# Five edits of a static job list in a two-layer transformer step: loads and transposes at the start, one late turn of layer 0, the boundary of the layers, who splits twelve weight quarters, and where the last gate's sigmoid stands

## The chip, the cores and the metric

The kernel runs on one core of a Trainium2 chip. The metric is the device time in microseconds (us), as the median of several runs. TensorE (PE in the rows) multiplies and transposes, with its weight loads as PEld; VectorE is DVE, ScalarE is ACT, GpSimd is POOL, and SyncE (SP) issues nearly all transfers.

## What is computed

One inference step of two layers over 512 tokens of a new stream and 8 x 16 tokens of running streams, in float32, with D_MODEL 1024. The first layer has latent attention and differential attention side by side; the second has stick-breaking attention.

```
def _even_layer(x, pos, caches, prm, lam_init):
    h = x @ w_in
    q_lat, ckv, krope, g_mla, dq, dk, dv, g_diff = _split_cols(h, EVEN_SECTIONS)
    ...
    o = jnp.concatenate([o_mla * jax.nn.silu(g_mla), o_diff * jax.nn.silu(g_diff)], axis=-1) @ w_out
    y = _layernorm(ALPHA * x + o, ln_g, ln_b)

def _odd_layer(x, pos, caches, prm):
    q, k, v, g = _split_cols(x @ w_in, (SB_W, SB_W, SB_W, SB_W))
    ...
    o = (o.reshape(b, s, SB_W) * jax.nn.silu(g)) @ w_out
    y = _layernorm(ALPHA * x + o, ln_g, ln_b)

def _sb_core(q, k, v, qpos, kpos):
    z = jnp.einsum('bqhd,bkhd->bhqk', q, k).astype(jnp.float32) * (SB_HD ** -0.5)
    valid = kpos[None, :] < qpos[:, None]
    log_beta = jax.nn.log_sigmoid(z)
    log_rem = jnp.where(valid, jax.nn.log_sigmoid(-z), 0.0)
    later = lax.cumsum(log_rem, axis=3, reverse=True) - log_rem
    a = jnp.where(valid, jnp.exp(log_beta + later), 0.0).astype(v.dtype)
```

## The kernel before

`make_schedule()` writes one list of jobs, a tuple for each. Every engine walks the same list from start to end and does its share of each job, in the order of the list, so a job that waits on an engine holds back all that stands behind it on that engine. Semaphores join the engines. Tokens stand in five tiles of 128: 0 to 3 the prompt, 4 (`S_TILE`) the running streams.

**Products.** A float32 factor is split into a high part (a cast on ACT) and the rest (a subtraction on DVE); a product is three matmuls (high by high, low by high, high by low, line L932). `("xT", layer, t, h)` transposes half h of tile t: four transposes on TensorE (L970), the cast of all four on ACT (L1335), the subtraction on DVE (L1569), which sets the PSUM bank free.

**Weights.** They come in 144 quarters of 128 x 2 x 256 or 128 x 512 words, through three stage buffers. `("cvt", n)`: SP loads quarter n, ACT casts it into `w_hi` (L1345), DVE subtracts into `w_lo` (L1575), and only then does SP load quarter n + 3 in its place. Quarters 128 to 143 are the second layer's output weights, `out100`, `out110`, `out101`, `out111`: the last two digits are the half of the 1024 input rows (k) and the half of the output columns. `w_hi` and `w_lo` hold two sections, so a section may be overwritten only when its last reader is done (`upper_read` is such a flag).

**Banks.** `assign_banks` deals out PSUM banks along the list: `turn0`, `turn1`, `value0`, `proj0` in a ring for most jobs; `pair0` and `pair1` (two banks each) for the attention scores; and `begin` jobs take theirs from a ring of four, which are the two banks of `pair0` (`score0`, `score1`) and the two of `pair1` (`turn2`, `proj1`). A bank is taken when its last user is `drained`.

**Output projections.** `("out", layer, first, t, h)` multiplies tile t with half h of the output weights, in eight k blocks of three matmuls; `("begin", layer, t)` does the first four blocks of the right half ahead. DVE adds the bank to `x_sb` (L1812, L1817); `ln` is then four DVE instructions (L1821 statistics, L1832, L1833, L1835), a power on GpSimd (L905) and the scaling with it on DVE (`shift`, L1846).

**Attention of layer 1.** A step of `stick_pipeline` is the scores of a few heads on a pair of banks, ACT's log-sigmoids (L1435 to L1437), a masked product, scan and product on DVE (L1683, L1687, L1689; the last one drains the pair), ACT's exponential (L1442), transposes on TensorE (`turn`, L1147), and the product with the values. `fills` are the other jobs laid between the steps. `("sig", g, 1)` is ACT's sigmoid of a gate's second half, in three activations of 128 x 640 (L1534 to L1536), and `sigm` the product on DVE and one more activation (L1869, L1540).

## Time and profile before

| | |
|---|---|
| median of 3 runs | 869.32 us (866.99 to 869.53) |
| the profiled execution | 869.3 us, its span 867.5 us |
| TensorE busy | 829.4 us, 96% |
| VectorE, ScalarE, GpSimd busy | 527.5, 413.0, 63.5 us |
| mean granted clock of TensorE | 0.991 |

Each row of a timeline gives the start in us from the span's start, the time taken in us, the engine, the line and operation, what is written and read, the count of alike instructions in a row, and in brackets the idle time ahead and what ended it. Instructions of one engine overlap a little, so the distance of their starts is less than their durations.

### The profile page before, as it was taken

The page shows a single profiled execution, that of the slowest core. Times are in us where ns is not written, and L with a number is a line of the kernel's source. Part 1 is how long each engine was busy: PE and PEld are TensorE (multiplying, and loading weights), DVE is VectorE, ACT ScalarE, POOL GpSimd, SP SyncE. Part 2 cuts the span into 40 slices and gives each one's busy share as a digit, 9 for nine tenths or more (in the row PEclk, how much of TensorE's full clock was granted, in tenths as well). Part 3 has the DMA queues.
Part 4 walks back from the last instruction along what each step waited for, and adds up shares of the span by engine and source line. Part 5 has one row for each costly group of instructions (what it writes and reads, how often), then busy time and mean ns, then how long its engine had stood idle before and what let it go on. Part 6 is the DMA issues. An engine that isn't in the chain of part 4 may idle for free.

```text
span 867.5 us, 17101 instructions
## 1 busy us (share of the span) xinstructions
PE 829.4 (96%) x6676; PEld 707.8 (82%) x6676; DVE 527.5 (61%) x1056; ACT 413.0 (48%) x945; POOL 63.5 (7%) x94
## 2 busy tenths in 40 slices
PE   6999999999999999999999999999999999999994
PEld 6996687878888888677899998888888888877673
DVE  3265346655565657667833466666566776777867
ACT  4233443343444456432224555754675555785710
POOL 2120000000000000001210010001000100000002
PEclk9999999999999999999999999999999999998998
DMA  6631212211323333413133334233333333343203
GB/s 225 152 105 50 61 44 65 64 39 31 129 65 106 105 100 134 139 59 138 49 117 104 117 104 136 88 105 117 114 99 100 118 130 111 100 136 106 73 22 121
DMA packets 67389, 86.25 MB, mean 99 GB/s; under 512 B 6000, under 2 KB 53904, under 8 KB 67312
## 3 DMA queue, kind: packets, MB, share of 16 engines
q1 hardware_dynamic: 63568, 74.47, 27.1%
q0 software_dynamic: 3744, 10.70, 3.9%
q8 instruction: 55, 0.90, 0.4%
q14 instruction: 22, 0.18, 0.1%
HBM read 74.25 MB, written 10.90 MB: 98 GB/s over the span
## 4 chain that ended last, share of the span: by engine, by line
PE 71%; issue 18%; DVE 4%; ACT 3%; POOL 2%; DMA 1%; DVEq 0%; SPq 0%; POOLq 0%; ACTq 0%
PE turn L932 25%; PE pair L932 14%; PE value L932 13%; PE proj L932 11%; PE turn L970 2%; POOL rstd L905 2%; PE turn L1147 1%; PE proj L970 1%; PE value L970 1%; DVE w_lo L1575 1%; PE value L1147 1%; PE proj L1147 1%; PE pair L970 1%; DMA x_sb<-in_x_prompt_dram 0%; ACT w_hi L1345 0%
## 5 line engine op out<-in xcount | busy, mean ns | idle before, releaser
L1575 DVE TENSOR_TENSOR w_lo<-stage,w_hi 128x512 fp32r<-128x512 f32 (+1 forms) x144 | 97.0, 682 | 109.1 <-ACT w_hi L1345 108.9
L932 PE MATMUL turn<-w_hi,xT_hi 128*128 128x256 f32 (+2 forms) x406 | 127.3, 314 | 0.3 <-DVE x_sb L1817 0.3
L932 PE MATMUL turn<-w_hi,xT_lo 128*128 128x256 f32 (+2 forms) x406 | 123.2, 303 | 0.0
L932 PE MATMUL turn<-w_lo,xT_hi 128*128 128x256 f32 (+2 forms) x406 | 123.1, 303 | 0.0
L1345 ACT CAST w_hi<-stage 128x512 fp32r<-128x512 f32 (+1 forms) x144 | 87.2, 615 | 30.0 <-PE turn L932 8.5
L932 PEld LDWEIGHTS turn<-w_hi,xT_hi 128*128 128x128 f32 x406 | 78.1, 192 | 3.6 <-DVE x_sb L1817 0.5
L932 PEld LDWEIGHTS turn<-w_hi,xT_lo 128*128 128x128 f32 x406 | 77.9, 192 | 3.1
L932 PEld LDWEIGHTS turn<-w_lo,xT_hi 128*128 128x128 f32 x406 | 78.2, 193 | 2.7
L932 PE MATMUL value<-w_hi,xT_hi 128*128 128x256 f32 (+2 forms) x196 | 62.8, 320 | 3.0 <-DVE w_lo L1575 3.0
L1425 ACT ACTIVATE work<-pair,peak 128x512 f32<-128x512 f32 (+4 forms) x80 | 41.0, 517 | 45.5 <-DVE peak L1676 45.4
L1687 DVE TENSOR_TENSOR_SCAN probs<-probs 128x512 f32<-128x512 f32 (+4 forms) x80 | 60.9, 794 | 1.6
L932 PE MATMUL value<-w_lo,xT_hi 128*128 128x256 f32 (+2 forms) x196 | 59.9, 306 | 0.0
L932 PE MATMUL value<-w_hi,xT_lo 128*128 128x256 f32 (+2 forms) x196 | 59.9, 305 | 0.0
L932 PE MATMUL turn<-xT_hi,w_hi 128*128 128x320 f32 x176 | 56.0, 318 | 0.0
L932 PE MATMUL turn<-xT_hi,w_lo 128*128 128x320 f32 x176 | 54.4, 309 | 0.0
L932 PE MATMUL turn<-xT_lo,w_hi 128*128 128x320 f32 x176 | 54.4, 309 | 0.0
L932 PE MATMUL proj<-w_hi,xT_hi 128*128 128x256 f32 (+2 forms) x150 | 46.4, 309 | 2.1 <-DVE w_lo L1575 1.3
L932 PE MATMUL proj<-w_lo,xT_hi 128*128 128x256 f32 (+2 forms) x150 | 44.7, 298 | 0.0
L932 PE MATMUL proj<-w_hi,xT_lo 128*128 128x256 f32 (+2 forms) x150 | 44.7, 298 | 0.0
L932 PEld LDWEIGHTS value<-w_hi,xT_hi 128*128 128x128 f32 x196 | 38.1, 195 | 6.2 <-issue 3.1
L1435 ACT ACTIVATE probs<-pair 128x272 f32<-128x272 f32 (+4 forms) x48 | 28.8, 600 | 26.5 <-PE pair L932 26.2
L932 PE MATMUL pair<-w_hi,xT_hi 128*128 128x256 f32 (+2 forms) x128 | 40.4, 316 | 0.8 <-DVE xT_lo L1569 0.8
(527 smaller groups left out, 2024.5 us busy)
## 6 DMA issues: line engine op xcount, KB each, us to landing
stage<-in_w_in_odd_dram SPq DMA_DIRECT2D x64, 256.0 KB, 2.6
stage<-in_w_in_even_dram SPq DMA_DIRECT2D x44, 256.0 KB, 2.8
k_c<-in_cache_sb_k_dram SPq DMA_DIRECT2D x32, 256.0 KB, 3.4
v_c<-in_cache_sb_v_dram SPq DMA_DIRECT2D x32, 256.0 KB, 2.9
x_sb<-in_x_prompt_dram SPq DMA_DIRECT2D x8, 512.0 KB, 4.3
mlaK<-in_cache_diff_k_dram SPq DMA_DIRECT2D x8, 512.0 KB, 3.9
mlaK<-in_cache_diff_v_dram SPq DMA_DIRECT2D x8, 512.0 KB, 4.4
stage<-in_w_out_even_dram SPq DMA_DIRECT2D x16, 256.0 KB, 2.7
```

Of the source, the lines that this page charges most:

```text
L905: nc.gpsimd.tensor_tensor(rstd[:, i, :], mv[:, i, 1:2], minus_half[:, 0:1], ALU.pow).then_inc(pow_out, 1)
L932: return nc.tensor.matmul(o, l, r, start=first, stop=last)
L970: i = nc.tensor.transpose(ps(job)[0:c, c0:c0 + r], src, ident[0:r, 0:r])
L1147: m = nc.tensor.transpose(ps(job)[0:kn, j * P:(j + 1) * P], p[:, k0:k0 + kn], ident[:, :])
L1345: nc.scalar.copy(piece(w_hi[:, sec % 2, k * 512:(k + 1) * 512]), piece(stage[:, n % STAGES, :])).then_inc(hi_done, 1)
L1425: e = nc.scalar.activation(prob(s, i), ps(score)[:, i, 0:width(s)], ACT.Exp, bias=peak[:, r, i:i + 1], accum_out=total[:, r, i:i + 1])
L1435: link(nc.scalar.activation(e, z, ACT.Abs))
L1575: v.tensor_tensor(piece(w_lo[:, sec % 2, words]), piece(stage[:, n % STAGES, :]), piece(w_hi[:, sec % 2, words].bitcast(F32)), ALU.subtrac ...
L1687: i = v.tensor_tensor_scan(c, c, c, 0.0, ALU.add, ALU.max)
```

## The change

1. Start. Tile 0 of the input is loaded as left half, weight quarter 0, right half (with a semaphore of its own, `x_right_in`), quarters 1 and 2, in place of whole tile, quarters 0, 1, 2. The list goes `xT 0 0 0`, `cvt 0`, `xT 0 0 1` in place of both `xT` first. The projection `A` of every tile waits for the transposed right half only at its fifth k block.
2. Turn 42 of layer 0. `cvt 51` and `mcvt 4` (the cast and the subtraction of the fourth output operand, L1349 and L1580) stand behind turn 43's work.
3. Boundary of the layers. `begin` for tiles 0, 1 and 4 now comes first; `ln` and `shift` of the tiles are interleaved with the projections; four `xT` stand in a row ahead of `out 0 2 3 1`, and those of tiles 2 and 3 come behind `k 0 0` and `k 0 1`. `upper_read` is given by `last_lower`, which is `out 0 2 3 1`.
4. Splits. For quarters 128 to 139 the subtraction is GpSimd's, into the same `w_lo`.
5. `sig 3 1` stands one turn later.

```
+POOL_SPLITS = range(QUARTERS * (len(SECTIONS) - 4), QUARTERS * (len(SECTIONS) - 1))
...
-    jobs = layer0(0) + first + [("A", 0, 0)] + layer0(1)
+    jobs = [("xT", 0, 0, 0)] + first[:1] + [("xT", 0, 0, 1)] + first[1:] + [("A", 0, 0)] + layer0(1)
...
-        fills[i].append(bundle)
+        fills[i].append(bundle if i < 42 else bundle[:1])
...
-            fills[i].append([("mcvt", bundle[0][1])])
+            fills[i if i < 42 else i + 1].append([("mcvt", bundle[0][1])] + (bundle[1:] if i == 42 else []))
...
-    jobs += finish(0) + finish(1) + layer1(0) + finish(2) + layer1(1) + finish(3) + coming[:1] + layer1(2) + coming[1:] + finish(S_TILE)
+    jobs += [("begin", 0, 0), ("begin", 0, 1), ("begin", 0, S_TILE), ("out", 0, 2, 0, 1), ("ln", 0, 0), ("out", 0, 2, 1, 1)]
+    jobs += [("shift", 0, 0), ("ln", 0, 1), ("shift", 0, 1), ("out", 0, 2, 2, 1), ("ln", 0, 2)] + layer1(0) + layer1(1)
+    jobs += coming[:1] + [("shift", 0, 2)] + coming[1:3] + [("out", 0, 2, 3, 1)] + coming[3:] + [("ln", 0, 3)]
+    jobs += [("out", 0, 2, S_TILE, 1), ("shift", 0, 3), ("ln", 0, S_TILE), ("shift", 0, S_TILE)]
...
-            keys = [[("k", g, 0)] + layer1(3), [("k", g, 1), ("kT", g, 0)],
+            keys = [[("k", g, 0)] + layer1(2), [("k", g, 1), ("kT", g, 0)] + layer1(3),
...
-              [six[0], [("ocvt", 3), ("sig", g, 1)]], [[("sigm", g, 1)], six[1] + [("ocvt", 2), ("silu", g, 1)] + second[2:]],
+              [six[0], [("ocvt", 3)]], [[("sig", g, 1)], [("sigm", g, 1)] + six[1] + [("ocvt", 2), ("silu", g, 1)] + second[2:]],
...
+        def wait_split(eng, n):
+            if n in POOL_SPLITS:
+                eng.wait_ge(pool_cvt_done, n - POOL_SPLITS.start + 1)
+            else:
+                eng.wait_ge(cvt_done, n + 1 - (len(POOL_SPLITS) if n >= POOL_SPLITS.stop else 0))
...
+            sp.dma_start(x_sb[:, 0, 0:D // 2], x_p[:, 0, 0:D // 2]).then_inc(x_in[0], 16)
+            load_quarter(0)
+            sp.dma_start(x_sb[:, 0, D // 2:], x_p[:, 0, D // 2:]).then_inc(x_right_in, 16)
...
+                elif kind == "cvt" and job[1] in POOL_SPLITS:
+                    n = job[1]
+                    sec, words = n // QUARTERS, slice(n % QUARTERS * 512, (n % QUARTERS + 1) * 512)
+                    pool.wait_ge(hi_done, n + 1)
+                    nc.gpsimd.tensor_tensor(w_lo[:, sec % 2, words], stage[:, n % STAGES, :],
+                                            w_hi[:, sec % 2, words].bitcast(F32), ALU.subtract).then_inc(pool_cvt_done, 1)
...
+                        if job[0] == "A" and k == KD // 2:
+                            wait_drained(pe, ("xT", 0, t, 1))
```

Line numbers of the changed kernel are higher by 19 to 21 for the lines named here (L932 becomes L951, L970 L991, L1147 L1167, L1569 L1589, L1846 L1866).

TensorE at the boundary, before: behind `out 0 2 1 1` on `turn0` stand the transposes of tile 0, then `out 0 2 2 1` on `proj0`, the transposes of tile 1, and `out 0 2 3 1` on `value0`.

```order
L970 MATMUL turn1<-ident,x_sb 128x128 [waits drained_turn1,ln_done]
L970 MATMUL value0<-ident,x_sb 128x128 [waits drained_value0,ln_done]
L932 MATMUL proj0<-w_hi,xT_hi 128x512 [waits ocvt_done,drained_proj0,drained_turn1]
L970 MATMUL turn0<-ident,x_sb 128x128 [waits drained_turn0,ln_done]
L970 MATMUL turn1<-ident,x_sb 128x128 [waits drained_turn1,ln_done]
L932 MATMUL value0<-w_hi,xT_hi 128x512 [waits ocvt_done,drained_value0,drained_proj0]
```

The same place after the change, from `out 0 2 2 1` on `proj0` on.

```order
L951 MATMUL proj0<-w_hi,xT_hi 128x512 [waits ocvt_done,drained_proj0,drained_turn1]
L991 MATMUL turn0<-ident,x_sb 128x128 [waits drained_turn0,ln_done]
L991 MATMUL turn1<-ident,x_sb 128x128 [waits drained_turn1,ln_done]
L991 MATMUL value0<-ident,x_sb 128x128 [waits drained_value0,ln_done]
L991 MATMUL proj0<-ident,x_sb 128x128 [waits drained_proj0,ln_done]
L951 MATMUL turn0<-w_hi,xT_hi 128x512 [waits ocvt_done,drained_turn0,drained_proj0]
```

Four transposed halves now use all four banks of the ring in a row, and `out 0 2 3 1` takes `turn0` again, the first of them.

VectorE at that place after the change, from the addition of `out 0 2 2 1` to that of `out 0 2 3 1`.

```order
L1832 SCALAR_TENSOR_TENSOR x_sb<-x_sb,proj0 128x512 [waits filled_proj0,xres_in2]
L1841 BN_STATS bn<-x_sb 128x6 [waits drained_proj0]
L1852 BN_AGGR mv<-bn 128x2 [waits stats_done,drained_proj0,drained_turn1]
L1853 TENSOR_SCALAR mv<-mv 128x1 [waits dve_step]
L1855 SCALAR_TENSOR_TENSOR x_sb<-x_sb,mv,lat 128x1024 [waits gains_in]
L1589 TENSOR_TENSOR xT_lo<-turn0,xT_hi 128x4x128 [waits xhi_done]
L1589 TENSOR_TENSOR xT_lo<-turn1,xT_hi 128x4x128 [waits xhi_done]
L1589 TENSOR_TENSOR xT_lo<-value0,xT_hi 128x4x128 [waits xhi_done]
L1589 TENSOR_TENSOR xT_lo<-proj0,xT_hi 128x4x128 [waits xhi_done]
L1595 TENSOR_TENSOR w_lo<-stage,w_hi 128x512 [waits hi_done]
```

The subtraction that drains `turn0` now stands behind all five instructions of tile 2's `ln`.

TensorE late in layer 1 before: the transposes and value products of the last steps but one, then `begin 1 3`, the last of the five `begin` jobs.

```order
L1147 MATMUL value0<-ident,probs1 128x128 [waits stick_done,drained_value0]
L970 MATMUL proj0<-ident,probs1 128x128 [waits drained_proj0,stick_done]
L932 MATMUL turn0<-work8,v_n 64x128 [waits drained_proj0,drained_turn1,drained_value0,drained_turn0]
L932 MATMUL turn0<-work8,v_n 64x128 [waits drained_turn1]
L932 MATMUL pair0<-w_hi,xT_hi 128x512 [waits cvt_done,ocvt_done,drained_pair0]
```

After the change:

```order
L1167 MATMUL proj0<-ident,probs1 128x128 [waits stick_done,drained_proj0]
L991 MATMUL turn0<-ident,probs1 128x128 [waits drained_turn0,stick_done]
L951 MATMUL turn1<-work8,v_n 64x128 [waits drained_turn0,drained_value0,drained_proj0,drained_turn1]
L951 MATMUL turn1<-work8,v_n 64x128 [waits drained_value0]
L951 MATMUL pair1<-w_hi,xT_hi 128x512 [waits pool_cvt_done,ocvt_done,drained_pair1]
```

The three `begin` jobs of layer 0 have turned the ring of four by three places: `begin 1 3` now takes a bank of `pair1`, on which the last step's scores (`B`, tile 3) stand, and not one of `pair0`.

## Rows read from the trace of the kernel before

**Rows 1.** The page's engines: busy us, share of the span, instructions.

```profile
PE 829.4 (96%) x6676; PEld 707.8 (82%) x6676; DVE 527.5 (61%) x1056; ACT 413.0 (48%) x945; POOL 63.5 (7%) x94
```

**Rows 2.** Waits of TensorE: what waited for what, us in all, times, longest.

```profile
PE turn L1147 <- ACT probs L1442: 2.5, 1, 2.5
...
PE pair L932 <- DVE probs L1689: 0.6, 1, 0.6
```

**Rows 3.** Timeline of the start.

```profile
1.17 0.42 SPq L721 DMA_DIRECT2D x_sb<-in_x_prompt_dram  x1
...
4.96 1.94 PE L970 MATMUL turn<-ident,x_sb 128*128 128x128 f32 x8 [4.96 <-DMA x_sb<-in_x_prompt_dram]
...
6.94 0.59 ACT L1335 CAST xT_hi<-turn 128x512 fp32r<-128x512 f32 x1 [0.27 <-PE turn L970]
...
8.17 1.89 DVE L1575 TENSOR_TENSOR w_lo<-stage,w_hi 128x512 fp32r<-128x512 f32 x3
...
8.99 0.55 PE L932 MATMUL value<-w_hi,xT_hi 128*128 128x256 f32 x1 [2.09 <-DVE w_lo L1575]
...
16.52 0.36 PE L932 MATMUL pair<-w_hi,xT_hi 128*128 128x256 f32 x1 [0.78 <-DVE xT_lo L1569]
```

**Rows 4.** Transfers of the first 20 us: GB/s in slices of 0.5 us.

```profile
GB/s 0 0 0 57 197 303 270 324 326 291 270 277 416 375 451 180 57 8 0 23 139 371 295 369 328 254 287 344 270 360 381 353 357 326 145 27 65 247 124 2
```

**Rows 5.** Timeline, turn 42 of layer 0.

```profile
350.21 0.68 DVE L1575 TENSOR_TENSOR w_lo<-stage,w_hi 128x512 fp32r<-128x512 f32 x1
...
351.41 0.16 DVE L1694 RECIPROCAL coef<-total 128x2 f32<-128x2 f32 x1
...
353.22 0.52 PE L970 MATMUL turn<-ident,mlaK 128*128 128x128 f32 x3 [1.59 <-DVE probs L1722]
```

**Rows 6.** Timeline of the boundary of the layers.

```profile
401.12 0.50 PE L932 MATMUL proj<-w_hi,xT_hi 128*128 128x512 f32 x1 [1.28 <-DVE w_lo L1575]
...
402.19 0.69 DVE L1812 SCALAR_TENSOR_TENSOR x_sb<-x_sb,proj 128x512 f32<-128x512 f32 x1 [1.12 <-PE proj L932]
...
405.85 1.28 DVE L1846 SCALAR_TENSOR_TENSOR x_sb<-x_sb,rstd,lat 128x1024 f32<-128x1024 f32 x1 [0.52 <-POOL rstd L905]
...
408.17 0.48 PE L932 MATMUL proj<-w_hi,xT_hi 128*128 128x512 f32 x1
...
413.73 1.03 PE L970 MATMUL turn<-ident,x_sb 128*128 128x128 f32 x8
...
435.40 0.36 PE L932 MATMUL proj<-w_hi,xT_hi 128*128 128x256 f32 x1 [0.58 <-DVE xT_lo L1569]
```

**Rows 7.** Timeline around the last gate's sigmoid.

```profile
778.68 0.75 ACT L1534 ACTIVATE probs<-gT 128x640 f32<-128x640 f32 x1
...
781.59 0.87 PE L1147 MATMUL turn<-ident,probs 128*128 128x128 f32 x3 [2.54 <-ACT probs L1442]
```

**Rows 8.** Windows: length, busy us of PE, PEld, DVE, ACT, POOL, granted clock, DMA share, GB/s.

```profile
781.00:787.00 6.00, 5.41 (x15) 4.30 (x16) 4.24 (x4) 4.42 (x11) 0.00 (x0) 0.50 0.18 50
...
819.00:821.00 2.00, 0.86 (x11) 0.55 (x10) 1.56 (x6) 2.00 (x6) 0.00 (x0) 1.00 0.55 191
855.00:859.00 4.00, 0.17 (x1) 0.00 (x0) 3.93 (x7) 0.00 (x0) 1.51 (x1) 1.00 0.32 131
```

**Rows 9.** Timeline late in layer 1, around `begin 1 3`.

```profile
816.11 1.15 ACT L1345 CAST w_hi<-stage 128x512 fp32r<-128x512 f32 x2
...
820.28 0.66 PE L932 MATMUL turn<-work,v_n 128*64 128x128 f32 x8 [1.14 <-DVE x_sb L1817]
...
821.82 0.50 PE L932 MATMUL pair<-w_hi,xT_hi 128*128 128x512 f32 x1
...
824.15 0.42 DVE L1689 TENSOR_TENSOR probs<-pair,probs 128x256 f32<-128x256 f32 x1
```

**Rows 10.** GpSimd's groups by form: busy us, mean ns; idle ahead.

```profile
L905 POOL TENSOR_TENSOR rstd<-mv,minus_half 128x1 f32<-128x1 f32 x10 | 15.2, 1516 | 174.3 <-DVE mv L1833 174.3
...
L873 POOL TENSOR_TENSOR ss<-ss,minus_half 128x10 f32<-128x10 f32 x1 | 2.0, 1995 | 24.3 <-DVE ss L1596 24.3
```

More of the change, by code:

```diff
@@ L272, in make_schedule @@
     jobs += [("stats", 0, S_TILE, 0), ("stats", 0, 0, 0)] + upper[2:]
-    def finish(t):
-        return [("out", 0, 2, t, 1), ("ln", 0, t), ("shift", 0, t)]
     def layer1(t):
@@ L549, in trunk_kernel @@
         x_in = [sem(f"x_in{t}") for t in range(TILES)]
+        x_right_in = sem("x_right_in")
         gains_in, gains1_in = sem("gains_in"), sem("gains1_in")
@@ L552, in trunk_kernel @@
         hi_done, cvt_done = sem("hi_done"), sem("cvt_done")
+        pool_cvt_done = sem("pool_cvt_done")
         xhi_done = sem("xhi_done")
@@ L662, in trunk_kernel @@
         stick_no = {s: i + 1 for i, s in enumerate(sb_steps)}
+        last_lower = [j for j in schedule if j[0] == "out" and j[1] == 0 and j[4] == 1 and ("begin", 0, j[3]) not in where][-1]
         by_act = [s for s in sb_steps if s[1] == GROUPS - 1]
@@ L718, in _ @@
             sp.dma_start(ident[:, :], a["c_ident"]).then_inc(consts_in, 16)
-            for t in range(TILES):
+            sp.dma_start(x_sb[:, 0, 0:D // 2], x_p[:, 0, 0:D // 2]).then_inc(x_in[0], 16)
+            load_quarter(0)
+            sp.dma_start(x_sb[:, 0, D // 2:], x_p[:, 0, D // 2:]).then_inc(x_right_in, 16)
+            for n in range(1, STAGES):
+                load_quarter(n)
+            for t in range(1, TILES):
                 src = x_p[:, t, :] if t < PT_TILES else x_s
                 sp.dma_start(x_sb[:, t, :], src).then_inc(x_in[t], 16)
-                if t == 0:
-                    for n in range(STAGES):
-                        load_quarter(n)
                 if t == 1:
@@ L763, in _ @@
                 if kind == "cvt" and 0 < job[1] < QUARTERS * len(SECTIONS) - STAGES:
-                    sp.wait_ge(cvt_done, job[1] + 1)
+                    wait_split(sp, job[1])
                     load_quarter(job[1] + STAGES)
@@ L951, in wait_quarter @@
                 if units[sec][0] == job:
-                    pe.wait_ge(cvt_done, QUARTERS * SECTIONS.index(sec) + quarter + 1)
+                    wait_split(pe, QUARTERS * SECTIONS.index(sec) + quarter)
             def project(job, t):
@@ L979, in _ @@
                     if layer == 0:
-                        pe.wait_ge(x_in[t], 16)
+                        pe.wait_ge(x_right_in if t == 0 and h == 1 else x_in[t], 16)
                     else:
@@ L984, in _ @@
                 elif kind == "A":
-                    for h in range(2):
-                        wait_drained(pe, ("xT", 0, job[1], h))
+                    wait_drained(pe, ("xT", 0, job[1], 0))
                     project(job, job[1])
@@ L1256, in _ @@
                         m = product(ps(job)[:, :], x_block(k, tok(t)), w_block(sec, k % 4 * 512, 512), k == ks[0], k == ks[-1])
-                        if k == 3 and job == units["out011"][1]:
+                        if k == 3 and job == last_lower:
                             m.then_inc(upper_read, 1)
@@ L1569, in _ @@
                     v.tensor_tensor(dst(xT_lo), src, dst(xT_hi).bitcast(F32), ALU.subtract).then_inc(done, 1)
-                elif kind == "cvt":
+                elif kind == "cvt" and job[1] not in POOL_SPLITS:
                     n = job[1]
```

## Prediction

> **What bounds the kernel now.** I read the page's engines first: TensorE is busy 829.4 us of 867.5, 96% [rows 1]. So the sum of matmuls is the time, and a change that alters no matmul, as this one, can only move TensorE's idle time. The chain of waits lists that idle time. Its largest single waits are 4.96 us for the first tile and 2.09 us after it [rows 3], 2.5 us for ACT's exponential ahead of a `turn` (2.54 in the timeline) [rows 2, 7], 1.59 us in layer 0's turn 42 [rows 5], 1.28 us at the boundary of the layers [rows 6] and 1.14 us late in layer 1 [rows 9]. Each edit aims at one or two of them. I went to each place in the timeline, walked VectorE's list with the rows' durations, and asked what TensorE then waits for. Last I read the granted clock by windows, because one of the waits costs more than its length: it was 0.50, the 1.2 GHz level, over 781:787, while TensorE was busy 5.41 us [rows 8]. Half of that work time, 2.7 us, is lost on top of the wait.
>
> The span stands 1.8 us below the profiled execution's 869.3 us, and that execution is the median of the runs to within 0.1 us; I add changes to 869.3.
>
> **Start: gain 2.0 (1.2 to 2.4).** The first tile's transfer is issued at 1.17 and TensorE begins at 4.96 [rows 3]. Transfers ran at about 300 GB/s there [rows 4], so the 256 KB that are no longer waited for are worth 0.85 us. Then `A` waited for the split of quarter 0, which ACT and DVE did behind the right half: ACT's second cast is at 6.94 and the first weight split on DVE at 8.17 [rows 3]. With the weight in the right half's place the split can end at about 8.15 in place of 8.85: another 0.85 earlier, with a split of 0.63 (a third of the three in a row) behind a cast of like length. `A` begins 1.7 us earlier. Part of this may go on the split of quarter 1 (0.25 us or more, since it and the right half follow each other on both engines), and the matmuls' slow pace of the first microseconds may last as long as before, which leaves 1.0 to 1.7. Then the 0.78 us before `A` of tile 1 [rows 3] shrink by one split half, about 0.7, since that job needs the right half only at its fifth block. Low end: bandwidth is shared and only 0.5 comes, plus 0.7.
>
> **Turn 42: gain 1.2 (0.9 to 1.5).** DVE does two splits from 350.21 to 351.41 ahead of the softmax's small instructions and the copies that TensorE waits for until 353.22 [rows 5]. Both go behind. 1.2 of the 1.59 us go. The weight they make is read late enough: TensorE does the next turn's transposes first.
>
> **Boundary: loss 1.0 (gain 0.5 to loss 2.0).** A projection of 24 matmuls takes 5.5 us (408.17 to 413.73) [rows 6], a half 2.73. Three `begin` jobs of 12 matmuls cover the 1.28 us wait for the last split [rows 6], and two short waits in `k 0 0` for late quarters of weight go too, since they are loaded earlier against TensorE's place. But the order shown above makes TensorE wait for VectorE. Walk: the begins end at 403.0, tile 0's rest at 405.7, tile 1's at 408.5, tile 2's whole product at 413.9. From a filled bank to the last scaling DVE now needs 5.0 us (402.19 to 405.85 and 1.28 more) [rows 6], GpSimd's 1.5 us among them [rows 10]. With two tiles 2.7 us apart these interleave: DVE does tile 1's scaling until 415.1, tile 2's addition, statistics and `ln` from 415.1 to 418.1, and then the split that drains `turn0`, 418.1 to 418.7. TensorE has finished its 16 transposes at 416.1 and `out 0 2 3 1` wants `turn0`: a new wait of 2.5 us, and 0.4 in small pieces among the transposes. Before, the same product had `value0`, long drained. Then 5.45 + 2.73 us of projections, `k 0 0`, transposes, `k 0 1` bring TensorE to 433.8; the next transposes want `value0`, whose split stands behind `ln` and `shift` of tiles 3 and 4, at 435.4: another 1.6 us. `k 0 2` begins at 436.4 against 435.40 [rows 6]. If DVE's pieces pack a little tighter than my walk the loss is nil or a small gain.
>
> **The gate's sigmoid: gain 4.0 (3.0 to 4.7).** ACT's three activations of 0.75 us, 778.68 to 781.0, stand ahead of the exponential for which TensorE waits until 781.59 [rows 7]. Gone, the exponential starts 2.25 us earlier, the wait is 0.3, and the clock has no reason to fall: 2.25 + 2.7 = 4.95. From this goes a new wait: `sigm` and `out 1 0 1 0`'s addition on DVE now stand behind the 128 x 1024 scans of the step after, and the next values want that bank, about 1.0 us. The moved activations do not hold the next exponential: the scans end later than they do.
>
> **Splits on GpSimd: gain 0.5, and some of the 1.14.** VectorE loses 12 splits of 0.68 us [rows 5]. It is on TensorE's path in only two places: 0.6 us ahead of scores [rows 2] and the 1.14 us [rows 9], where DVE's additions and splits precede. GpSimd's own price p for 128 x 512 is not in the trace. From below it is bound by VectorE's 0.68 [rows 5], and the nearest rows above are GpSimd's power operation, 1.5 us for one element and 2.0 for ten [rows 10], a dearer operation on fewer elements. I take the middle, 1.3, and anywhere from 0.7 to 2.0 the sum is the same: quarters 136 and 137 can start when ACT's casts of 816.11 end, at 816.7 and 817.3, 138 and 139 only from 820.5 [rows 9], and `begin 1 3` needs the last at 825.7. Up to p = 2.25 all four (816.7 + 4p) are in time.
>
> The Trainium skill, GPSIMD Engine Reference, section "Elementwise — side-by-side cycle accounting", gives an add of two tensors as 1.96 times VectorE's time. By that p would be an estimated 1.3 us, and the sum stays; no run here shows it yet.
>
> **The bank of `begin 1 3`: loss 2.1 (1.5 to 2.6).** This follows from the boundary's three jobs. It started at 821.82 on `pair0`, while the last step's scores stood on `pair1` until DVE's last product, 824.15 to 824.57 [rows 9]. It must now wait for exactly that. With the 1.14 us wait mostly gone it is ready at about 821.2; DVE, rid of its two splits there, ends the step at about 823.6. A wait of 2.4 us; against before it begins 1.8 to 2.1 us late. Nothing after it gives this back, as TensorE is dense from there to 855.
>
> **Sum and clock.** 2.0 + 1.2 - 1.0 + 4.0 + 0.5 - 2.1 = 4.6: 864.7 us if the clock never falls. But there are two new waits of 2.4 to 2.5 us, as long as the one before which it fell, with only transposes or narrow matmuls around. Against it: 1.14 us of wait with 0.86 us of work in 819:821 left it at 1.00, and so did 3.8 us of idle in 855:859 [rows 8]. That is undecided from these rows, so I give each about even odds. A fall costs 2.0 to 2.7 us. Likeliest is one of two: 864.7 + 2.3 = **867.0 us**. Its own range is 865.2 to 868.8.
>
> **Rivals.**
> - No fall (25%): 864.7 us. For it: the clock held through 855:859.
> - One fall (38%): 867.0.
> - Both fall (17%): 869.3, no change in sum; for it: the wait at 781.59 had the same length and the same kind of work ahead of it.
> - The boundary works as its order suggests (8%): DVE interleaves better, both waits shrink to under 0.5 us, and the boundary gains 2: 862.5 us. Against it: the split that drains `turn0` stands behind a 1.28 us instruction that cannot end before 418.
> - VectorE and GpSimd hold each other up (7%): late in layer 1 GpSimd's four subtractions run while DVE does splits of `oT` and scans whose operands are both in SBUF. If each such instruction waits for a GpSimd one of about 1.3 us at two places, the step that frees `pair1` ends about 1.3 us later: 867.0 + 1.3 = 868.3 us. No row shows the two together. The Trainium skill, SBUF — State Buffer, section "Who interferes with whom", says that a DVE instruction with two SBUF inputs contends with a GpSimd instruction that reads SBUF; no run here shows it yet.
> - Slower (5%): GpSimd's price. If p is above 2.25 us, `begin 1 3` waits for quarter 139, four microseconds of delay for each microsecond of p. To end at 871.9 us, from 867.0, takes 4.9 us more, so p = 3.5. It decides from there; the ten-element power, at 2.0, is below it. Columns are 512 here, which speaks for it.
>
> **The range and chances.** 863.0 to 870.5 us holds all but the slow tail of the last rival and the far ends of the sums. A measurement of this kernel can tell 0.3%, 2.6 us, from no change: faster is under 866.7, slower over 871.9. No fall and the good boundary are faster (33%), and 12 of the 38% of one fall; the rest of it, the lock and most of two falls are the same; slower are 5% for GpSimd and 5% for two falls with poor ends of the sums. So 0.45, 0.45, 0.10.
>
> **What would show it.** Start: `A` begins at 7.3. Turn 42: the wait at 353.22 is under 0.5. Boundary: a wait of about 2.5 us of TensorE on `turn0` for `xT_lo` L1589, and 1.6 us later for the same line; granted clock in the windows behind it. Sigmoid: no wait over 0.5 for L1462, clock 1.00 throughout, a wait near 1.0 for `x_sb`. Tail: `begin 1 3` on `pair1` released by `probs` L1709 with 2.4 us. GpSimd: twelve rows near 1.3 us. I am wrong if the granted clock stays at full level in all of these, or if GpSimd's rows exceed 2.3 us.

## The result: a quarter of a percent slower, and the profile after

The changed kernel takes 870.72 us (median of 14 runs, 869.83 to 871.89), the one before 868.73 us in the same 14 rounds. The ratio is 1.0025, with a 95% interval of 1.0015 to 1.0034: slower, by about 2 us, where 867.0 was forecast and 870.5 was the upper end of the range. The profiled execution took 870.0 us, its span 868.2.

TensorE's own row on the page of after (as [rows 1]):

```profile
PE 831.4 (96%) x6676; PEld 709.2 (82%) x6676; DVE 524.4 (60%) x1044; ACT 413.3 (48%) x945; POOL 80.3 (9%) x106
```

The count of matmuls is the same, and yet TensorE is busy 2.0 us more than in [rows 1]. More busy time for the same matmuls can only be slower matmuls; the windows below show where. VectorE has 12 instructions less but only 3.1 us less busy time, where 12 splits of 0.68 are 8.2 us.

The chain of waits of after, TensorE's largest (us in total, times, longest), against [rows 2]:

```profile
PE turn L991 <- DMA x_sb<-in_x_prompt_dram: 4.8, 2, 4.2
PE pair L951 <- DVE probs L1709: 2.6, 1, 2.6
PE turn L951 <- issue: 2.4, 1, 2.4
...
PE value L951 <- DVE x_sb L1837: 2.0, 2, 1.7
...
PE value L991 <- DVE xT_lo L1589: 1.4, 1, 1.4
```

Of the waits at which the change aimed all but the last are shorter; the lower four here are new or have grown. The timeline of after shows where, with the start of each to be held against [rows 3], [rows 5], [rows 6], [rows 7] and [rows 9]:

```profile
4.21 1.09 PE L991 MATMUL turn<-ident,x_sb 128*128 128x128 f32 x4 [4.21 <-DMA x_sb<-in_x_prompt_dram]
5.91 1.11 PE L991 MATMUL turn<-ident,x_sb 128*128 128x128 f32 x4 [0.61 <-DMA x_sb<-in_x_prompt_dram]
7.39 0.55 PE L951 MATMUL value<-w_hi,xT_hi 128*128 128x256 f32 x1 [0.36 <-DVE w_lo L1595]
15.16 0.39 PE L951 MATMUL pair<-w_hi,xT_hi 128*128 128x256 f32 x1
350.66 0.63 PE L991 MATMUL turn<-ident,mlaK 128*128 128x128 f32 x4 [0.39 <-DVE probs L1742]
415.32 1.28 DVE L1589 TENSOR_TENSOR xT_lo<-turn,xT_hi 128x512 fp32r<-128x512 f32 x2
416.11 0.76 PE L951 MATMUL turn<-w_hi,xT_hi 128*128 128x512 f32 x1 [2.38 <-issue]
434.27 0.63 PE L991 MATMUL value<-ident,x_sb 128*128 128x128 f32 x4 [1.45 <-DVE xT_lo L1589]
778.53 0.52 PE L1167 MATMUL turn<-ident,probs 128*128 128x128 f32 x3 [0.38 <-ACT probs L1462]
785.03 0.88 PE L951 MATMUL value<-work,v_n 128*64 128x128 f32 x12 [0.90 <-DVE x_sb L1832]
811.92 2.65 POOL L916 TENSOR_TENSOR w_lo<-stage,w_hi 128x512 fp32r<-128x512 f32 x2 [23.07 <-ACT w_hi L1365]
812.31 2.54 DVE L1707 TENSOR_TENSOR_SCAN probs<-probs 128x128 f32<-128x128 f32 x2
815.96 0.66 PE L951 MATMUL value<-work,v_n 128*64 128x128 f32 x8 [1.70 <-DVE x_sb L1837]
819.65 0.42 DVE L1709 TENSOR_TENSOR probs<-pair,probs 128x256 f32<-128x256 f32 x1
820.13 0.80 PE L951 MATMUL pair<-w_hi,xT_hi 128*128 128x512 f32 x1 [2.56 <-DVE probs L1709]
825.40 0.39 PE L951 MATMUL value<-w_hi,xT_hi 128*128 128x512 f32 x1
```

The row at 416.11 names no releaser ("issue"), but the split that drains `turn0` is the first of the two at 415.32 and ends at about 416.0. Windows of after (columns as [rows 8]) behind the two longest waits:

```profile
416.00:419.00 3.00, 2.89 (x7) 2.34 (x8) 1.80 (x4) 0.00 (x0) 0.00 (x0) 0.50 0.00 0
...
820.00:825.00 5.00, 4.87 (x12) 3.85 (x13) 0.41 (x2) 0.42 (x1) 0.00 (x0) 0.50 0.18 52
```

The granted clock is 0.50 in both, the 1.2 GHz level; the fall behind the gate's sigmoid in [rows 8] has become two.

**The account.** How far ahead of before TensorE is at the same job, in the two profiled executions (start before less start after), shows where each microsecond went:

| place | before | after | ahead by | step |
|---|---|---|---|---|
| `A` of tile 0 | 8.99 | 7.39 | 1.60 | |
| `A` of tile 1 | 16.52 | 15.16 | 1.36 | start +1.36 |
| behind turn 42 | 353.22 | 350.66 | 2.56 | turn 42 +1.20 |
| a value product, layer 1 | 537.66 | 537.51 | 0.15 | boundary -2.41 |
| transposes ahead of the gate's sigmoid | 776.67 | 775.77 | 0.90 | GpSimd ahead of scores +0.75 |
| `out 1 0 3 0` | 791.67 | 786.78 | 4.89 | sigmoid +3.99 |
| `value` behind the 1.70 us wait | 820.28 | 815.96 | 4.32 | GpSimd late in layer 1 -0.57 |
| `begin 1 3` | 821.82 | 820.13 | 1.69 | bank -2.63 |
| the product behind it | 824.69 | 825.40 | -0.71 | clock -2.40 |

The sum, -0.71, is the difference of the two spans (867.5 and 868.2). The medians differ by 2.0 us: the profiled execution of before is 0.6 us over its median, that of after 0.7 us under its own. The experiments show what varies from one execution to the next (the start, and the clock).

### The profile page after: what moved, and what is told of

Same layout as the page of the kernel before. It is cut to its first block, busy times and chain, and to the rows that moved or that the text cites. A ratio compares the mean times of both kernels' runs of the same rounds, so it can differ in the third digit from the quotient of the medians.

```text
span 868.2 us, 17103 instructions
## 1 busy us (share of the span) xinstructions
PE 831.4 (96%) x6676; PEld 709.2 (82%) x6676; DVE 524.4 (60%) x1044; ACT 413.3 (48%) x945; POOL 80.3 (9%) x106
## 4 chain that ended last, share of the span: by engine, by line
PE 80%; issue 6%; DVE 6%; ACT 4%; POOL 2%; DMA 0%; DVEq 0%; SPq 0%; POOLq 0%; ACTq 0%
PE turn L951 28%; PE value L951 17%; PE pair L951 16%; PE proj L951 11%; PE turn L991 2%; PE proj L991 2%; POOL rstd L924 1%; PE turn L1167 1%; PE value L991 1%; DVE probs L1707 1%; PE proj L1167 1%; PE value L1167 1%; DVE w_lo L1595 1%; DVE x_sb L1866 1%; ACT w_hi L1365 1%
## 5 line engine op out<-in xcount | busy, mean ns | idle before, releaser
L951 PE MATMUL turn<-w_hi,xT_hi 128*128 128x256 f32 (+2 forms) x356 | 109.2, 307 | 2.4 <-issue 2.4
L951 PE MATMUL turn<-w_hi,xT_lo 128*128 128x256 f32 (+2 forms) x356 | 105.7, 297 | 0.0
L951 PE MATMUL turn<-w_lo,xT_hi 128*128 128x256 f32 (+2 forms) x356 | 105.7, 297 | 0.0
L951 PE MATMUL value<-w_hi,xT_hi 128*128 128x256 f32 (+2 forms) x236 | 75.0, 318 | 0.6 <-DVE w_lo L1595 0.4
L951 PEld LDWEIGHTS turn<-w_hi,xT_hi 128*128 128x128 f32 x356 | 68.3, 192 | 4.5 <-issue 2.6
L951 PE MATMUL value<-w_lo,xT_hi 128*128 128x256 f32 (+2 forms) x236 | 71.5, 303 | 0.0
L951 PE MATMUL value<-w_hi,xT_lo 128*128 128x256 f32 (+2 forms) x236 | 71.5, 303 | 0.0
L951 PEld LDWEIGHTS turn<-w_lo,xT_hi 128*128 128x128 f32 x356 | 68.4, 192 | 1.8
L951 PEld LDWEIGHTS turn<-w_hi,xT_lo 128*128 128x128 f32 x356 | 68.2, 192 | 1.9
L951 PE MATMUL pair<-w_hi,xT_hi 128*128 128x256 f32 (+2 forms) x152 | 50.8, 334 | 2.7 <-DVE probs L1709 2.6
L951 PE MATMUL turn<-xT_hi,w_hi 128*128 128x320 f32 x160 | 50.8, 318 | 0.0
L951 PE MATMUL pair<-w_lo,xT_hi 128*128 128x256 f32 (+2 forms) x152 | 49.9, 328 | 0.0
L951 PE MATMUL pair<-w_hi,xT_lo 128*128 128x256 f32 (+2 forms) x152 | 49.8, 328 | 0.0
L951 PEld LDWEIGHTS value<-w_hi,xT_hi 128*128 128x128 f32 x236 | 46.1, 196 | 4.1 <-DVE xT_lo L1589 0.7
L951 PE MATMUL turn<-xT_hi,w_lo 128*128 128x320 f32 x160 | 49.4, 309 | 0.0
L951 PE MATMUL turn<-xT_lo,w_hi 128*128 128x320 f32 x160 | 49.4, 309 | 0.0
L951 PEld LDWEIGHTS value<-w_lo,xT_hi 128*128 128x128 f32 x236 | 46.2, 196 | 1.3
L951 PEld LDWEIGHTS value<-w_hi,xT_lo 128*128 128x128 f32 x236 | 46.0, 195 | 1.5
```

The lines of the kernel that those rows point to most:

```text
L951: return nc.tensor.matmul(o, l, r, start=first, stop=last)
```

## The experiments

Twelve kernels in three sets; each ratio is against the kernel before in the same set, with its 95% interval. Those named a_ are the changed kernel with something undone, b_ the kernel before with one part alone, and best_first and c_ the changed kernel mended. The kernel before took 869.23 us in the set of a_, 868.48 in the set of b_start, b_turn, b_sig and b_bound, and 868.47 in that of b_shift, best_first and c_. The changed kernel is compared by its own ratio, 1.0025.

**a_ring: the bank of `begin 1 3` alone put back.**

```
+            key = (slots, job[1]) if job[0] == "begin" else slots
-            n = turns.get(slots, 0)
+            n = turns.get(key, 0)
```

> The changed kernel, with only the bank ring of the begin jobs counted anew for layer 1, so that begin 1 3 stands on pair0 as before the change. Theory 1 (the bank wait and the clock that falls behind it): begin 1 3 starts near 817.6 in place of 820.13, which gives 2.5 us, and its 12 matmuls run at 0.23 us in place of 0.43, which gives 2.4 more: about 4.9 us less than the changed kernel, near 865.8. Rival (the clock has another cause, such as the waits before it): only 2.5 us less, near 868.2, with slow matmuls still there. Rival 2 (the wait is replaced by a wait for GpSimd's split of quarter 139): under 1.5 us less.

Measured: 866.21 us, ratio 0.9963 (0.9948 to 0.9978). That is 3.0 us under the kernel before, where the changed kernel is 2.0 over it: 5.0 us between them. Its timeline there:

```profile
817.57 0.66 PE L952 MATMUL value<-work,v_n 128*64 128x128 f32 x8 [1.69 <-DVE x_sb L1838]
...
819.11 0.50 PE L952 MATMUL pair<-w_hi,xT_hi 128*128 128x512 f32 x1
819.45 0.39 PE L952 MATMUL pair<-w_lo,xT_hi 128*128 128x512 f32 x1
...
821.97 0.39 PE L952 MATMUL value<-w_hi,xT_hi 128*128 128x512 f32 x1
```

`begin 1 3` follows the value products at once and takes 2.86 us (819.11 to 821.97), where it took 5.27 after the change (820.13 to 825.40): 2.4 us by the clock. From the value product to `begin 1 3` it is 1.54 us, where it was 4.17: 2.6 us by the wait. Theory 1 holds: one bank, a side effect of three jobs 400 us earlier, costs the wait and the clock.

**b_shift: the kernel before, with that ring alone started three places on.**

```
-            n = turns.get(slots, 0)
+            n = turns.get(slots, 3 if job[0] == "begin" else 0)
```

> The kernel before, with nothing changed but the begin jobs' ring started three places on, so that begin 1 3 stands on pair1. Theory 1: begin 1 3 waits for the last step's product on VectorE, some 2.7 us (824.57 in place of 821.82), and the clock falls behind the wait for another 2.4: 5 us slower, near 874. Rival (the wait alone, no fall): 2.7 us slower. Rival 2 (nothing, since VectorE ends its step as early as TensorE comes): under 0.5.

Measured: 873.08 us, ratio 1.0050 (1.0035 to 1.0064), 4.6 us over the kernel before, as theory 1 had it (5 us). Its timeline, and one window of TensorE's (columns as [rows 8]):

```profile
823.74 0.80 PE L953 MATMUL pair<-w_hi,xT_hi 128*128 128x512 f32 x1 [2.74 <-DVE probs L1710]
```

```profile
823.00:828.00 5.00, 4.26 (x10) 3.40 (x11) 0.98 (x3) 0.42 (x1) 0.00 (x0) 0.50 0.17 53
```

From the other side the same: a bank number, with no instruction added or moved, is worth 4.6 us by the medians, 2.7 of it the wait and the rest the clock.

**a_dve: the changed kernel with all splits on VectorE.**

```
-POOL_SPLITS = range(QUARTERS * (len(SECTIONS) - 4), QUARTERS * (len(SECTIONS) - 1))
+POOL_SPLITS = range(0)
```

> The changed kernel, with all twelve splits back on VectorE. Theory 1 (VectorE and GpSimd hold each other up, and what VectorE is spared it loses again): VectorE's scans that took 2.54 us return to 0.74 and the splits come back, so the last step's end on VectorE and with it the time stay within 0.7 us of the changed kernel. Rival (the splits on GpSimd are a relief, as predicted): 0.5 to 1.2 us slower than the changed kernel. Rival 2 (the lock costs more than the splits): 1 us or more faster.

Measured: 870.76 us, ratio 1.0023 (1.0010 to 1.0036), no difference to the changed kernel's 1.0025, which fits theory 1; the two intervals are too wide to leave out a rival's 0.5 us, so the traces have to say it. The twelve splits on GpSimd took, by form:

```profile
L916 POOL TENSOR_TENSOR w_lo<-stage,w_hi 128x512 fp32r<-128x512 f32 x12 | 16.8, 1416 | 82.5 <-ACT w_hi L1365 82.5
```

One pair of them in the trace of after, and a VectorE product that ran beside it:

```profile
785.73 3.12 POOL L916 TENSOR_TENSOR w_lo<-stage,w_hi 128x512 fp32r<-128x512 f32 x2 [12.27 <-ACT w_hi L1365]
785.76 1.93 DVE L1895 TENSOR_TENSOR gT<-gT,probs 128x640 f32<-128x640 f32 x1
```

Without GpSimd's splits the timeline of a_dve has:

```profile
788.52 0.82 DVE L1895 TENSOR_TENSOR gT<-gT,probs 128x640 f32<-128x640 f32 x1
...
814.65 1.29 DVE L1595 TENSOR_TENSOR w_lo<-stage,w_hi 128x512 fp32r<-128x512 f32 x2
...
816.31 0.74 DVE L1707 TENSOR_TENSOR_SCAN probs<-probs 128x128 f32<-128x128 f32 x2
...
818.16 0.66 PE L951 MATMUL value<-work,v_n 128*64 128x128 f32 x8 [1.13 <-DVE x_sb L1837]
```

The same two scans take 0.74 us here and 2.54 with GpSimd's splits beside them; in the changed kernel they end at 814.85, just after GpSimd's two, which end at 814.57. So VectorE is spared 1.2 us of splits and made to wait 1.8. This is what the Trainium skill, SBUF — State Buffer, section "Who interferes with whom", says of a DVE instruction with two SBUF inputs beside a GpSimd instruction that reads SBUF; the trace agrees, 2.54 against 0.74, and 1.93 against 0.82 for the 128 x 640 product, for which TensorE did not wait. The gain is elsewhere: from 733.44 to 780.16 in a_ring, 46.72 us, against 47.45 (733.84 to 781.29) in a_dve, 0.73 us for the splits ahead of one set of scores. GpSimd gives 0.7 in one place and takes 0.6 in the other. The last step does not end later for it: from the value product to `begin 1 3` it is 4.36 us here and 4.17 after the change, so with GpSimd's last two splits the step ends 0.2 us sooner behind the product, where they took 1.3 on VectorE; beside them, in the trace of after, its two scans take 1.16 us in place of 0.74.

**a_ring_dve: both.** The edits are the two above.

> The changed kernel with both: the ring of layer 1 as before the change, and the splits on VectorE. Theory 1: as the ring alone, within 0.7 us, since the 1.14 us wait for an addition on VectorE comes back and the 1.70 us one with GpSimd goes. Rival: GpSimd's splits cost 1 us or more once the bank's wait no longer hides it, and this is the faster of the two by that.

Measured: 865.25 us, ratio 0.9954 (0.9937 to 0.9971), 1.0 us under a_ring by the medians. That lies between theory 1 (within 0.7) and the rival (1 or more), and the intervals overlap, so neither is shown. In the traces the value product behind GpSimd's splits comes 0.55 us sooner than in a_ring, counted from the wait behind the gate's sigmoid (817.08 less 786.72, and 817.57 less 786.66), as it does between a_dve and the changed kernel.

**a_oldbound: the changed kernel with the old order at the boundary** (its four lines, and the two `keys` lines, as before the change).

> The changed kernel, with the old order at the boundary of the layers (no begin jobs in layer 0, so begin 1 3 is on pair0 again). Theory 1: it gives back the boundary's loss of 2.4 us, 1.2 of it by the clock, and the tail's 4.9: near 863.4. Rival (the boundary's waits only move later, where TensorE waits less): the tail's 4.9 alone, near 865.8.

Measured: 864.85 us, ratio 0.9953 (0.9938 to 0.9969). The interval, 863.8 to 866.5 us, holds the rival's 865.8 and not theory 1's 863.4. By the medians it is 1.4 us under a_ring, which has the new order, and the intervals overlap; in the profiled executions the stretch from turn 42 to a value product late in layer 1 takes 379.1 us (351.32 to 730.44) against 381.3 (352.11 to 733.44), 2.2 us less, as theory 1 has it. What is missing of it in the time is in the clock, which fell in this profiled execution behind a wait of 1.69 us, and did not in a_ring's behind the same wait. TensorE alone in a_oldbound (length, PE busy, granted clock, DMA share, GB/s):

```profile
817.00:818.00 1.00, 1.00 (x4) 0.50 0.76 190
```

So this run alone does not decide between the two; the next does.

**b_bound: the kernel before with the new boundary alone**, its ring counted anew as in a_ring.

> The kernel before, with the new order at the boundary of the layers alone, and layer 1's bank ring counted anew so that begin 1 3 stays on pair0. Theory 1: 2.4 us lost (waits of 2.4 and 1.4 us for splits on VectorE, and a clock fall that costs 1.2), near 871.2. Rival (as predicted): 1.0 us lost. Rival 2: the loss is caught up later, where TensorE waits for others: under 0.5.

Measured: 871.22 us, ratio 1.0026 (1.0016 to 1.0036), 2.7 us lost: theory 1's number, and the interval (1.4 to 3.1 us) leaves out both rivals. Its timeline has the same two waits as after:

```profile
418.72 0.77 PE L950 MATMUL turn<-w_hi,xT_hi 128*128 128x512 f32 x1 [2.38 <-issue]
436.83 0.63 PE L988 MATMUL value<-ident,x_sb 128*128 128x128 f32 x4 [1.46 <-DVE xT_lo L1587]
```

**b_start: the kernel before with the start's edit alone.**

> The kernel before, with the start's edit alone (tile 0 in halves, quarter 0 between them, A's late wait for the right half). Theory 1 (the right half's landing decides, and it comes anywhere from 5.9 to 7.2 us): the gain is 1.4 us where it lands early and near nothing where it lands late, so a median gain of 0.3 to 1.0 us. Rival (as predicted, 2.0 us): TensorE reaches the next tile's projection 2 us earlier in every run.

Measured: 866.83 us, ratio 0.9980 (0.9962 to 0.9998), 1.6 us by the medians; the interval, 0.2 to 3.3 us, holds theory 1 and the prediction's 2.0 both. That the right half's landing varies is seen in two other kernels with the same start; the second half's transposes, at 5.91 after the change, are here (a_ring, then a_dve):

```profile
7.01 1.11 PE L992 MATMUL turn<-ident,x_sb 128*128 128x128 f32 x4 [1.67 <-DMA x_sb<-in_x_prompt_dram]
```

```profile
7.23 1.11 PE L991 MATMUL turn<-ident,x_sb 128*128 128x128 f32 x4 [2.04 <-DMA x_sb<-in_x_prompt_dram]
```

Turn 42 is then reached at 352.11 and 352.53 in place of 350.66, 1.5 and 1.9 us later, behind a landing that was 1.1 and 1.3 us later. In b_start's own profile the half lands early (5.86), and `A` of tile 0 waits 0.96 us for the split of its last weight quarter instead. The fourteen traces together are the better measure. The first scores of layer 0 that wait for ACT's `vm` start at 103.3 to 105.9 us in the nine kernels with the new start (mean 104.6), and at 105.4 to 106.4 in the five with the old one (mean 105.9): 1.3 us gained on average, and anything from a loss of 0.5 to a gain of 3.1 for a pair taken at random.

**b_turn: the kernel before with turn 42's edit alone.**

> The kernel before, with the edit of layer 0's turn 42 alone. Theory 1: the wait of 1.59 us becomes 0.39 and TensorE keeps the 1.2 us to the end. Rival: later waits take them back, under 0.5 us gained.

Measured: 867.25 us, ratio 0.9990 (0.9974 to 1.0006), 1.2 us by the medians, which the interval can't tell from none or from the rival's. In its trace TensorE does keep the 1.2 us: from those first scores to the transposes behind the wait it is 246.59 us (106.23 to 352.82) against 247.81 before (105.41 to 353.22). The wait is 0.39 in its profile, too. This run showed something else. It still has the 2.54 us wait for ACT's exponential, and so has b_start. Windows of TensorE alone (length, PE busy, granted clock, DMA share, GB/s) behind it, before first, then b_turn and b_start:

```profile
780.00:781.00 1.00, 0.00 (x0) 0.85 0.48 165
```

```profile
781.00:782.00 1.00, 1.00 (x7) 0.99 0.78 258
782.00:783.00 1.00, 1.00 (x4) 0.50 0.01 4
...
785.00:786.00 1.00, 1.00 (x5) 0.80 0.00 0
786.00:787.00 1.00, 1.00 (x7) 1.00 0.00 0
```

```profile
780.00:781.00 1.00, 0.01 (x1) 1.00 0.34 71
...
783.00:784.00 1.00, 1.00 (x6) 1.00 0.00 0
```

The same wait lowered the clock to 0.50 from before its end in the kernel before [rows 8], only a microsecond behind its end in b_turn, and not at all in b_start. In time from the wait's end to the value product behind the 1.1 us wait: 38.7 us before (781.59 to 820.28), 37.5 in b_turn (780.78 to 818.29), 35.9 in b_start (780.99 to 816.91). The clock fell at the same wait in b_bound's and b_shift's profiles too, with 37.3 us in both. Whether it falls is thus a matter of the execution, and it costs 1.3 to 2.8 us where it does. It seems to fall in most: of the 64 executions of the kernel before that ran in these three sets, 16 have a mean granted clock of 0.994 or more and take 867.9 us or less; the other 48 have 0.993 or less and take 868.05 or more.

**b_sig: the kernel before with the sigmoid moved alone.**

> The kernel before, with the gate's sigmoid moved alone. Theory 1: the wait of 2.54 us becomes 0.4, the clock stays at 1.00 there, and 0.9 us go to the wait for an addition: 4.0 us gained, near 864.9. Rival (the clock falls anyway, a little later): 1.5 us gained or less.

Measured: 865.86 us, ratio 0.9966 (0.9955 to 0.9978): 2.6 us by the medians, 1.9 to 3.9 by the interval. The window shows the clock held:

```profile
781.00:787.00 6.00, 5.18 (x28) 4.18 (x27) 5.93 (x7) 4.50 (x9) 0.00 (x0) 1.00 0.28 91
```

The trace of after had given 4.0 us for it, against an execution of before in which the fall was at its dearest; against a median execution it is less. By its size it lies between the two theories, 1.4 us under the first and 1.1 over the rival; the mechanism is the first one's, since the clock did not fall. All its nine executions have a mean granted clock of 0.994 to 0.996 and lie within 2.1 us (865.52 to 867.59); the 29 of before in the same set have 0.991 to 0.995 and lie within 5.9 (866.56 to 872.43). The spread goes with the long wait and its clock.

**best_first: the changed kernel, old boundary, and only quarters 128 to 131 on GpSimd.**

```
+POOL_SPLITS = range(QUARTERS * (len(SECTIONS) - 4), QUARTERS * (len(SECTIONS) - 3))
```

> The changed kernel, with the old order at the boundary, and only quarters 128 to 131 split on GpSimd (136 to 139, where VectorE's scans wait for it, and 132 to 135 on VectorE). Theory 1 (GpSimd helps by 0.7 us ahead of the scores of step 758 and costs 0.5 in the tail): about 0.5 us under the kernel with all twelve there, near 864.3. Rival (the two are equal): 864.9.

Measured: 862.42 us, ratio 0.9932 (0.9919 to 0.9945), 2.4 us under a_oldbound by the medians. The two were in different sets (by the ratios it is 1.8 us) and the intervals are wide, so whether it is more than the 0.5 us expected is not shown; the wait at the place is 1.13 in place of 1.69, and the clock did not fall behind it.

**c_late1: the boundary mended by the bank.** The begins stay; tile 1's transposes go behind `out 0 2 3 1`; the ring as in a_ring, GpSimd as in best_first.

```
-    ... ("ln", 0, 2)] + layer1(0) + layer1(1)
-    jobs += coming[:1] + ... + [("out", 0, 2, 3, 1)] + coming[3:] + [("ln", 0, 3)]
+    ... ("ln", 0, 2)] + layer1(0)
+    jobs += coming[:1] + ... + [("out", 0, 2, 3, 1)] + coming[3:] + layer1(1) + [("ln", 0, 3)]
```

> The changed kernel, with layer 1's ring counted anew, quarters 128 to 131 alone on GpSimd, and tile 1's transposes moved behind out 0 2 3 1, which so takes value0 and not turn0. Theory 1 (the boundary lost by the four transposes in a row): the wait of 2.4 us goes and the clock does not fall there, about 2 us under the same kernel with the changed order: near 863.5. Rival (VectorE's list is what is late, and the time comes back as a longer wait of k 0 0 or k 0 2): no more than 0.5 us under it.

Measured: 861.90 us, ratio 0.9928 (0.9912 to 0.9944), which is no difference to best_first, the same with the old boundary, in the same set. The kernel from which theory 1 and the rival count, with the changed order and four splits on GpSimd, was not run. The wait for `turn0` is gone, but the timeline has the other one grown:

```profile
430.60 1.09 PE L992 MATMUL value<-ident,x_sb 128*128 128x128 f32 x4 [2.49 <-DVE xT_lo L1590]
```

and with it the clock fell, at the second place this time (0.60 in 430 to 432, 0.54 in 432 to 434). So the rival's mechanism holds in part: TensorE came to 430.6 earlier and waited for the same VectorE instruction, behind `ln` and `shift` of tiles 3 and 4.

**c_late2: and tile 2's transposes ahead of tile 4's `ln`.**

```
-    jobs += [("out", 0, 2, S_TILE, 1), ("shift", 0, 3), ("ln", 0, S_TILE), ...
+    jobs += [("out", 0, 2, S_TILE, 1), ("shift", 0, 3)] + layer1(2) + [("ln", 0, S_TILE), ...
-            keys = [[("k", g, 0)] + layer1(2), ...
+            keys = [[("k", g, 0)], ...
```

> As c_late1, and tile 2's transposes moved ahead of tile 4's ln, so that the split that drains value0 no longer stands behind ln and shift of tile 4. Theory 1: the second wait, 1.4 us, shrinks too: 0.5 to 1.5 us under c_late1. Rival: tile 4's scaling is then late for k 0 4 and takes it back.

Measured: 858.87 us, ratio 0.9890 (0.9877 to 0.9903), the fastest of all: 3.0 us under c_late1 by the medians (four executions). That is more than theory 1's 0.5 to 1.5. In the traces the boundary takes 2.7 us less than in c_late1, 1.8 of it by the wait (0.73 for 2.49); the rest goes with the fall of the clock. Timeline and window:

```profile
432.72 0.35 PE L952 MATMUL value<-w_hi,xT_hi 128*128 128x256 f32 x1 [0.73 <-DVE xT_lo L1590]
```

```profile
395.00:440.00 45.00, 44.04 (x276) 39.32 (x275) 32.61 (x52) 12.70 (x24) 10.13 (x10) 1.00 0.31 102
```

Both long waits are gone, the clock holds over the whole boundary, and TensorE idles 0.96 us of 45. From the transposes of `lat` ahead of the boundary to the value product behind it TensorE takes 149.5 us (382.35 to 531.89), against 152.0 before (385.64 to 537.66) and 154.4 after (383.08 to 537.51): a gain of 2.5 us where the change lost 2.4. So the begins were a good idea; what lost was which bank and which place in VectorE's list the transposes got.

## Why the prediction was wrong

The forecast was 2.3 us less than before; the medians say 2.0 us more. Of these 4.3 us, by the parts below, 1.5 are the second fall of the clock (3.8 us for two, where 2.3 was counted for one), 1.4 the sigmoid, 1.1 GpSimd and the bank late in layer 1, and about 0.5 the start; 0.25 went the other way. This is an estimate, since it mixes the profiled pair and medians.

**Start, predicted 2.0.** 1.36 in the profiled pair, 1.6 by b_start's median, 1.3 over the fourteen traces. `A` began at 7.39, as worked out (7.3). The step that was mis-sized is "matmuls' slow pace of the first microseconds may last as long as before": it did. Matmuls of 256 columns follow each other at 0.21 us until about 12.7 before and 12.9 after, and at 0.12 from there, so that of the 1.60 us only 0.67 were left at the next transposes (13.16 against 13.83), where 1.0 to 1.7 were allowed. And the right half's transfer, behind the left half and a weight quarter, lands anywhere from 5.7 to 7.2.

**Turn 42, predicted 1.2.** 1.20, by the wait's fall from 1.59 to 0.39.

**Boundary, predicted -1.0, clock aside.** -2.41 with the clock. The two waits are where the walk through VectorE's list put them, 2.38 and 1.45 us against 2.5 and 1.6. The window 416:419 at 0.50 is the rest: half of its 2.89 busy us is 1.4, and -1.0 and -1.4 are the -2.4. b_bound lost 2.7 by the medians.

**Sigmoid, predicted 4.0.** 3.99 in the pair, 2.6 by the medians of b_sig. The prediction took the fall of the clock in one execution, 2.7 us, as if each had it in full; it costs 0 to 2.8.

**GpSimd, predicted +0.5 and "some of the 1.14".** Price 1.42 us a split against an estimate of 1.3; +0.75 ahead of the scores. The second part failed: the wait grew from 1.14 to 1.70. It was among the rivals as the lock, with 7%; the scans were named rightly (of the `oT` splits one grew, from 0.42 to 0.77 us), and ahead of the value product it costs 0.57 us in place of 1.3.

**Bank, predicted -2.1.** -2.63. The 2.1 counted on VectorE, rid of two splits, ending the step 1.0 us earlier; it ended it 0.2 earlier (4.17 us behind the value product, against 4.36 in a_dve), since the lock took back 0.8 us (the scans 1.16 for 0.74, an `oT` split 0.77 for 0.42).

**Sum and clock: the step that failed.** "That is undecided from these rows, so I give each about even odds", and from it one fall of 2.3 us as the likeliest. Both fell, for 1.4 and 2.4 us, in the profiled execution of after, whose mean granted clock, 0.989, lies among those of its fourteen executions (0.987 to 0.990); the tail's also in the other two kernels profiled with that bank (a_dve, b_shift), the boundary's in all four others with the new order (a_ring, a_dve, a_ring_dve, b_bound). In the fourteen traces TensorE has fourteen waits of 2.4 to 2.7 us at these places and at the gate's sigmoid, and the clock fell at thirteen of them. The case of both had 17% and 869.3 us, no change; with the lock's 0.6 and 0.5 of the bank it is 1.1 us slower, of the 2.0 measured. The mistake was to read the idle microseconds at the end, 855:859 with the clock at 1.00, as a case against a fall. In the same trace of before the rows right behind it have the fall, with TensorE still idle:

```profile
859.00:860.00 1.00, 0.00 (x0) 0.00 (x0) 0.97 (x4) 0.00 (x0) 0.32 (x1) 0.60 0.00 0
860.00:864.00 4.00, 0.00 (x0) 0.00 (x0) 2.21 (x3) 0.00 (x0) 1.20 (x1) 0.50 0.59 232
```

And a_ring shows that the clock can be 1.00 through a wait and fall after it. At the boundary it waits 2.37 us until 417.56, and then has (TensorE alone):

```profile
417.00:418.00 1.00, 0.44 (x2) 1.00 0.00 0
418.00:419.00 1.00, 1.00 (x5) 0.52 0.00 0
```

The only mid-kernel wait of that length known from the trace of before had a fall. Two waits of the same length should have been priced like the one that was seen, not at half. Without the two new falls the parts of the profiled pair add up to 1.4 + 1.2 - 1.0 + 4.0 + 0.75 - 0.6 - 2.6 = 3.1 us of gain, where the prediction had 4.6; the falls took 1.4 and 2.4, more than all of it.

One number among the rivals does not come out of its own terms: with the boundary gaining 2 in place of losing 1, 864.7 becomes 861.7 without a fall and 864.0 with the tail's, and not 862.5. The boundary did not gain, so nothing hangs on it.

What stays open: what decides whether the clock falls in an execution, and when. A wait of 1.69 us was enough in a_oldbound and not in a_ring; 2.54 us was not in b_start.

## What to carry to other kernels

When jobs are added to a list from which banks are dealt in turn, every later user of that ring moves: look at who holds each bank afterwards, 400 us on as well, since one bank number was worth 4.6 us here. A wait of TensorE like these, 2.4 to 2.7 us, is to be priced with the fall of the clock that it mostly brings (1.3 to 2.8 us more in these runs), and removing it pays the same; look at the windows behind a wait as well as at the wait, before calling the clock unmoved. A new wait, somewhere else, takes back what was gained. And a product that takes the bank of the transposes just ahead waits for all that stands before their split on VectorE: another bank, or a place for the split ahead of the long instructions, turned a loss of 2.4 us into a gain of 2.5.

## What the runs showed of the hardware

The fall of TensorE's clock to the 1.2 GHz level comes at a different distance from the same wait in each execution: 0.9 us before its end (before), 1.2 behind it (b_turn), never (b_start). Of fourteen waits of 2.4 to 2.7 us in the traces thirteen had a fall, of two of 1.69 us with no other close behind one (a_oldbound, not a_ring). The mean granted clock parts the executions of the kernel before in two groups: 16 of 64 with 0.994 or more, none over 867.9 us, and 48 with less, none under 868.05.

VectorE's two scans of 128 x 128 took 2.54 us with two GpSimd subtractions beside them and 0.74 without, and a 128 x 640 product of two SBUF operands 1.93 in place of 0.82. GpSimd's subtraction of 128 x 512 took 1.42 us on average, 2.1 times VectorE's 0.68. Beside that product two of them took 3.12 us, and late in layer 1 two took 2.65.

The right half of the first tile, whose transfer stands behind the left half and a weight quarter, landed for TensorE at 5.7 to 7.2 us in nine executions with the same start.
